# A transformer step in two blocks on one core: recurrence by halves, fused attention maximum, earlier bias split, more held expert weights, first modulation by feature halves

## The chip, the cores and the metric

The kernel runs on one core of a Trainium2 chip. A core has a matrix engine (PE in the profile; its weight loads are PEld), a vector engine (DVE), an activation engine (ACT), a general engine (POOL) and a queue engine that issues transfers (SP, in the profile SPq). They run side by side and wait for each other by semaphores; 16 DMA engines move data between HBM and the on-chip memory. The metric is the device time of one execution in microseconds (us), less is better.

## The reference, cut to what matters

All data are float32, 256 tokens of 1024 features. The first block: modulation vectors from a condition, a projection to 2840 columns, two kinds of attention, a residual, and a mixture of 32 experts in which each token goes to four.

```python
mod = silu(c) @ ada_w + ada_b            # six vectors of 1024: shift, scale, gate, twice
h = rms_norm(x, ln1_g) * (1 + sc1) + sh1
z = h @ w_in                             # 1024 -> 2840
# compressed, selected and windowed attention on 8 heads, blockwise attention on 8 heads
s = softmax(q @ k.T * scale - slope * distance)
x = x + g1 * (concat(outputs) @ w_out)
u = h2[toks] @ w1[e] + b1[e]             # per expert; g_, lin = halves of u, clipped at 7
y = ((lin + 1) * g_ * sigmoid(1.702 * g_)) @ w2[e] + b2[e]
```

The second block puts 16 tokens ("meta") in front, so that it works on 272 columns, and has stick-breaking attention, an MLP, a gated linear recurrence and another MLP. The meta tokens are dropped at the end. The recurrence:

```python
gate = gelu(x @ w_in[:, :1024]);  u = causal_conv(x @ w_in[:, 1024:])
r, i = sigmoid(u @ w_rg + b_rg), sigmoid(u @ w_ig + b_ig)
log_a = (-8 * softplus(-lam)) * r;  a = exp(log_a)
bt = sqrt(-expm1(2 * log_a)) * (i * u)
h[t] = a[t] * h[t-1] + bt[t];  out = (h * gate) @ w_out
```

## The kernel before

Activations lie feature-major: a feature chunk of 128 on the partitions, tokens along the row. The program of each engine is written out by hand, in order, and nothing else sets the order. Every weight goes through a ring of four slots of 2 MB (`ring`), filled by SP in the order of `A_LOADS` (first block), then expert by expert, then `B_LOADS` (second block); SP waits until the slot's last reader is done before it issues the next load, and everything behind that load waits too.

**Front.** SP loads the condition `c`, `x`, and the modulation weights as four loads of 256 rows by 2048 columns (`ada`), then `w_in` in six column chunks. PE transposes `x`, multiplies modulation rows (L750), turns them (L758), and DVE makes the normalized, modulated input `hn` (L1608 to L1618). Only then does the projection begin: twelve products (v = 0 to 11, six chunks by two token halves, L795), each over all eight feature chunks. The first four need `w_in` columns 0 to 1023.

**Attention.** 12 units. For each, PE scores 768 columns into two PSUM banks (L885), DVE adds the distance bias into `scores` (L1742), takes four row maxima in two reductions (L1745, L1746), ACT exponentiates with them as bias (L1434), DVE makes factors from the sums (L1754 to L1760), POOL scales (L592), PE transposes (L895 to L899) and weighs the values (L914 to L919). Between these PE does the rest of the modulation (L750).

**Between attention and experts.** When the attention is done, SP loads held weights (L486) and ACT issues the loads of the expert biases. PE multiplies by `w_out` (L994), DVE adds the residual and makes the second `hn` (L1789, L1792), tokens are ranked, the first expert's rows are gathered (L1076). Meanwhile POOL splits the bias `b1` in three bfloat16 parts (L624 to L629); the first expert pass waits for that (`split_ready`).

**Experts.** A pass takes up to 64 tokens of an expert: PE adds the bias (L1111), multiplies four parts of `w1` (L1122, `w1_parts` counts them), gathers the next rows (L1076), scatters the last result (L1094), and multiplies two halves of `w2` (L1153). An expert has 12 MB of weights in six loads. Part 0 of experts 20, 24 and 28 does not come then: it has been loaded beforehand to a spare place, and POOL copies it into the ring slot. An expert with more than 64 tokens takes a second pass on the same weights.

**Recurrence.** PE makes eight recurrence inputs, the first gate input (L1316), 16 gate products (L1330), and then the other seven gate inputs (L1316), each of 272 columns. DVE, ACT and POOL make `a`, the square root and the gelu on whole tensors of eight chunks (128x2176) or on four (128x1088), DVE runs a scan per chunk (L2061) and gates it (L2070), and PE's output product (L1182, `dense`) waits for chunk k of the gated result at its k-th step (`lru_y`).

Of the kernel before, what the change touches and what calls it, by code (L numbers as in the profile page):

```python
# [33 lines left out]
BF16 = mybir.dt.bfloat16  # L34
# [6 lines left out]
P = 128  # L41
# [13 lines left out]
NEG = -1e30  # L55
FLAT = 30.0
# [13 lines left out]
A_LOADS = ([("ada", 0, k) for k in range(4)]  # L70
           + [("in", 0, c) for c in range(6)] + [("cmp", 0, 0)]
# [9 lines left out]
DMAS_OF = {"wout": 4, "gates": 2}  # L81
# [3 lines left out]
HELD = (20, 24, 28)  # L85
# [41 lines left out]
def a_freed(n):  # L127

    kind, layer, c = A_LOADS[n]
    return {"ada": ("mod_parts", 4 * layer + c + 1), "in": ("z_done", 2 * (c + 1)),  # L130
            "cmp": ("cmp_hidden", 1), "wout": ("wout_done", 4 * (c + 1))}[kind]
# [64 lines left out]
class Memory:  # L196

    def __init__(self, nc, ctx):
# [67 lines left out]
        self.OT = a.take(C, T)  # L267

# [30 lines left out]
        self.b2 = a.take(D)  # L299
        self.b1 = a.take(2, FF)  # L300
        self.b1parts = a.take(2, FF, dt=BF16)
# [21 lines left out]
        w2_at = ARENA - 864 - 2 * SLOT  # L323
        held_at = w2_at - len(HELD) * SLOT
        assert a.at <= held_at
        self.held = Area(arena, held_at).take(len(HELD), SLOT)
        self.w2 = Area(arena, w2_at).take(2, SLOT)
# [44 lines left out]
z_done z_copied doubled heads_ssq heads_root heads_normed gates_ready  # L372
# [3 lines left out]
scored biased maxed exped factored scaled flipped flipped_dve flipped_act o_parts o_copied  # L376
# [11 lines left out]
gate_tanh_in gate_tanh_in2 gate_tanh gate_tanh2 u_ready r_ready lam_in lam_out a_in a_exp mult_in mult_root lru_y  # L388
# [4 lines left out]
class Signals:  # L393

    def __init__(self, nc, ctx):
        self.sem = {name: ctx.enter_context(nc.semaphore(name)) for name in SEMAPHORES}
        self.loaded = [ctx.enter_context(nc.semaphore(f"loaded{s}")) for s in range(RING)]
        self.held_loaded = [ctx.enter_context(nc.semaphore(f"held_loaded{j}")) for j in range(len(HELD))]
# [6 lines left out]
def program_sync(nc, sp, m, s, a):  # L406
# [5 lines left out]
    def source(kind, layer, c):  # L412

        if kind == "ada":
            src = a["ada_w"][0, 2 * P * c:2 * P * (c + 1), 2048 * layer:2048 * (layer + 1)]
            return [(slice(0, P), 4096, 2048, src.rearrange("(k p) n -> p k n", p=P))]
        if kind == "in":
# [48 lines left out]
    for n, load_of in enumerate(A_LOADS):  # L466
        if n >= RING:
            wait_for(a_freed(n - RING))
        load(A_AT[n][0], load_of, s.loaded[A_AT[n][0]])
        if n == 0:  # L470
# [12 lines left out]
    def load_held(j):  # L483

        src = a["exp_w1"][0, HELD[j], 0:2 * P, :]
        sp.dma_start(m.held[:, j, :], src.rearrange("(p k) n -> p (k n)", p=P)).then_inc(s.held_loaded[j], 16)  # L486
# [12 lines left out]
    for part in range(PASS_LOADS):  # L499
# [6 lines left out]
        elif part == 4:  # L506
            sp.wait_ge(s["wout_done"], C)
# [12 lines left out]
    for held in HELD + (EXPERTS,):  # L520
        with sp.Fori(begin, held) as expert:
            load_expert(expert)
        if held < EXPERTS:
            load_expert(held, from_part=1)
        begin = held + 1

# [7 lines left out]
def program_gpsimd(nc, pool, m, s, a):  # L534
# [42 lines left out]
    for t in range(2):  # L577
        src = m.z[:, t, Z_KC:Z_KS].rearrange("p (g d) -> p g d", g=4).unsqueeze(2).to_broadcast([P, 4, 2, DH])
        g.tensor_copy(m.twice[:, t].rearrange("p g (c d) -> p g c d", c=2), src).then_inc(s["doubled"], 1)
    for u in range(UNITS):  # L580
        if u == 8:
            pool.wait_ge(s["heads_normed"], 5)
            pool.wait_ge(s["mod_ready"], 2)
# [32 lines left out]
    link(g.memset(m.wtile, 0.0))  # L616
    link(g.memset(m.b2[EXPERTS:64, :], 0.0))
    link(g.memset(m.b2[64:P, :], 0.0))
    g.memset(m.b1parts[96:P, :, :], 0.0).then_inc(s["pool_moe"], 1)
    pool.wait_ge(s["pool_moe"], 3)  # L620

    pool.wait_ge(s["bias_loaded"], 64)
    link(g.tensor_copy(m.b1parts[0:96, :, :], m.b1[0:96, :, :]))  # L624
    for q in (1, 2):
        for r in range(q, 3):
            rows = slice(32 * r, 32 * r + 32)
            link(g.tensor_tensor(m.b1[rows], m.b1[rows], m.b1parts[rows], ALU.subtract))
            last = g.tensor_copy(m.b1parts[rows], m.b1[rows])  # L629
            if (q, r) == (2, 2):  # L630
                last.then_inc(s["split_ready"], 1)
            else:
                link(last)
# [5 lines left out]
    for j, expert in enumerate(HELD):  # L639
# [3 lines left out]
        seen = m.b1[0:32, 0, 0:1]  # L643
        link(g.tensor_tensor(seen, seen, seen, ALU.subtract))
        pool.wait_ge(s.held_loaded[j], 16)
# [1514 lines left out]
```

## Time and profile before

| | us |
|---|---|
| median of 3 runs | 1906.66 (1902.97 to 1910.16) |
| profiled execution | 1906.46 |
| its span, first to last instruction | 1904.7 |
| PE busy | 1803.5 |
| DVE, ACT, POOL busy | 513.6, 252.6, 122.8 |

Busy time alone says little here: the stages have different limits. Times in the rows below are us from the start of the span. In a timeline row the numbers are the start, the length, the engine and line, the operation, what is written and read, the count, and in brackets how long the engine was idle before and what released it. The mean granted clock of PE is 0.991 of full.

### The profile page before, as it was taken

What the parts mean: (1) busy time and instruction counts of PE and PEld (TensorE: products, weight loads), DVE (VectorE), ACT (ScalarE), POOL (GpSimd) and SP (SyncE); (2) the same over time, 40 slices, a digit from 0 to 9 for tenths busy, and PEclk for the clock granted to TensorE, in tenths of its full rate; (3) what the DMA queues carried; (4) which work ended last, traced back from release to release, by engine and by line L of the source; (5) the groups of instructions that cost most, each with busy time, mean ns of one, the idle gap of its engine ahead of it and who ended that gap; (6) DMA issues with size and microseconds to landing.
All of it is one profiled execution on the core that took longest, in us unless ns stands there. A gap on an engine that the chain in (4) does not pass through costs nothing.

```text
span 1904.7 us, 21694 instructions
## 1 busy us (share of the span) xinstructions
PE 1803.5 (95%) x8583; PEld 1033.1 (54%) x8584; DVE 513.6 (27%) x1032; ACT 252.6 (13%) x519; POOL 122.8 (6%) x172
## 2 busy tenths in 40 slices
PE   6989899999999899899999989989999999899998
PEld 3545633333333333233333326867888888788887
DVE  1247532232313222222323313133110006611000
ACT  1125200011001001001001002022110003111000
POOL 3004500000000000100101001000000000200000
PEclk8999999999999999999999999999999999999999
DMA  9558899979999999999999997321344333434430
GB/s 361 178 229 266 320 407 428 428 305 428 428 428 429 428 429 427 428 429 428 429 428 428 428 428 289 133 89 45 133 158 152 133 132 111 176 133 160 150 132 23
DMA packets 93092, 547.38 MB, mean 287 GB/s; under 512 B 5906, under 2 KB 9186, under 8 KB 65298
## 3 DMA queue, kind: packets, MB, share of 16 engines
q1 hardware_dynamic: 92850, 545.75, 71.4%
q10 hardware_dynamic: 192, 0.92, 0.2%
q8 instruction: 37, 0.61, 0.1%
q14 instruction: 13, 0.11, 0.0%
HBM read 545.60 MB, written 1.05 MB: 287 GB/s over the span
## 4 chain that ended last, share of the span: by engine, by line
PE 66%; DMA 27%; DVE 4%; SPq 1%; issue 1%; POOL 1%; ACT 1%; DVEq 0%; POOLq 0%; ACTq 0%
DMA ring<-in_exp_w 26%; PE ps L1182 21%; PE ps L1122 13%; PE ps L1281 12%; PE ps L1153 5%; PE ps L795 4%; PE ps L1076 1%; PE ps L994 1%; PE ps L1094 1%; PE ps L1316 1%; PE ps L1233 1%; DMA ring<-in_w_in 1%; DVE arena L2061 1%; SPq L480 0%; PE ps L750 0%
## 5 line engine op out<-in xcount | busy, mean ns | idle before, releaser
L1122 PE MATMUL ps<-ring,arena 128*64 128x512 f32 x2112 | 470.7, 595 | 45.0 <-DMA ring<-in_exp_w 44.9
L1182 PE MATMUL ps<-hn,ring 128*128 128x272 f32 (+1 forms) x1536 | 346.5, 388 | 0.0
L1122 PEld LDWEIGHTS ps<-ring,arena 128*64 128x64 f32 x2112 | 150.0, 137 | 346.0 <-issue 247.1
L1182 PEld LDWEIGHTS ps<-hn,ring 128*128 128x128 f32 x1536 | 291.8, 190 | 53.3
L1153 PE MATMUL ps<-arena,hn 128*64 128x512 f32 x1056 | 233.9, 595 | 3.5
L1281 PE MATMUL ps<-arena,ring 128*128 128x272 f32 (+1 forms) x1024 | 228.5, 386 | 1.1 <-DVE arena L2011 1.1
L1281 PEld LDWEIGHTS ps<-arena,ring 128*128 128x128 f32 x1024 | 194.3, 190 | 35.0 <-DVE arena L2011 1.9
L1153 PEld LDWEIGHTS ps<-arena,hn 128*64 128x64 f32 x1056 | 75.3, 137 | 140.9 <-issue 140.6
L1912 DVE TENSOR_SCALAR sq<-ps 128x512 f32<-128x512 f32 x33 | 22.8, 692 | 346.9 <-PE ps L1122 346.9
L1824 DVE TENSOR_SCALAR sq<-arena,rstd 128x64 f32<-128x64 f32 x68 | 19.1, 324 | 304.3 <-PE ps L1122 303.6
L1362 ACT ACTIVATE hn<-ps 128x512 f32<-128x512 f32 (+1 forms) x99 | 52.0, 525 | 308.4 <-PE ps L1153 212.2
L1475 ACT ACTIVATE sq<-sq 128x512 f32<-128x512 f32 x33 | 20.8, 629 | 536.0 <-DVE sq L1912 536.0
L1951 DVE TENSOR_TENSOR xT<-ps,xT 128x272 f32<-128x272 f32 (+1 forms) x32 | 13.9, 433 | 261.8 <-PE ps L1281 217.9
L1843 DVE TENSOR_TENSOR arena<-ps,arena 128x512 f32<-128x512 f32 x132 | 81.5, 680 | 7.3 <-PE ps L1094 7.3
L795 PE MATMUL ps<-ring,hn 128*128 128x512 f32 (+1 forms) x192 | 78.5, 571 | 2.3 <-DMA ring<-in_w_in 2.3
L2011 DVE SCALAR_TENSOR_TENSOR arena<-ps,rstd 128x272 f32<-128x272 f32 (+1 forms) x64 | 27.5, 433 | 182.3 <-PE ps L1182 182.2
L676 POOL TENSOR_TENSOR sq<-sq 128x272 f32<-128x272 f32 (+1 forms) x34 | 25.4, 746 | 640.3 <-ACT sq L1495 639.8
L1094 PE MATMUL ps<-hn 64*128 64x512 f32 x264 | 65.6, 615 | 0.7 <-issue 0.7
L1182 PE MATMUL ps<-arena,ring 128*128 128x272 f32 (+1 forms) x256 | 59.6, 395 | 6.4 <-DVE arena L2070 5.8
L1076 PE MATMUL ps<-arena,sq 128*64 128x512 f32 x272 | 65.4, 601 | 0.0
L795 PEld LDWEIGHTS ps<-ring,hn 128*128 128x128 f32 x192 | 37.0, 194 | 42.6 <-issue 40.6
L1182 PEld LDWEIGHTS ps<-arena,ring 128*128 128x128 f32 x256 | 49.2, 194 | 16.4 <-DVE arena L2070 4.0
(365 smaller groups left out, 1231.1 us busy)
## 6 DMA issues: line engine op xcount, KB each, us to landing
ring<-in_exp_w SPq DMA_DIRECT2D x125, 2048.0 KB, 23.5
arena<-in_exp_w SPq DMA_DIRECT2D x67, 2048.0 KB, 21.6
ring<-in_mlp_w_up SPq DMA_DIRECT2D x16, 2048.0 KB, 7.5
ring<-in_mlp_w_down SPq DMA_DIRECT2D x16, 2048.0 KB, 7.8
ring<-in_ada_w SPq DMA_DIRECT2D x12, 2048.0 KB, 10.5
ring<-in_sb_w_qkv SPq DMA_DIRECT2D x6, 2048.0 KB, 14.0
ring<-in_w_in SPq DMA_DIRECT2D x5, 2048.0 KB, 11.0
ring<-in_lru_w_in SPq DMA_DIRECT2D x4, 2048.0 KB, 7.9
```

Of the source, the lines that this page charges most:

```text
L676: add = g.tensor_tensor(m.sq[:, 0, lo:TT], m.sq[:, 0, lo:TT], m.sq[:, c, lo:TT], ALU.add)
L795: last = mm(bank(v % 4)[:, 0:w], m.hn[:, k, META + P * t:META + P * t + P], wt[:, k, :], start=(k == 0), stop=(k == C - 1))
L1076: last = mm(bank(0)[64 * h:64 * h + 64, :], m.sel[:, t, :], m.h2[:, t, 512 * h:512 * h + 512], start=(t == 0), stop=(t == 1))
L1094: mm(bank(TOKEN_BANKS[n]), m.selz[rows, h, P * t:P * t + P], m.y[rows, :], start=True, stop=True).then_inc(s["scattered"], 1)
L1122: last = mm(bank(2 + part)[64 * h:64 * h + 64, :], lhs, w[:, k % 2, at:at + 512], start=False, stop=(k == C - 1))
L1153: last = mm(bank(5)[64 * h:64 * h + 64, :], m.aT[:, q, 64 * half:64 * half + 64], w[:, q, 512 * h:512 * h + 512], start=(half == 0 and q = ...
L1182: last = mm(bank((n0 + q) % 8)[:, lo:TT], w[:, k, P * q:P * q + P], act[:, k, lo:TT], start=(k == 0), stop=(k == C - 1))
L1281: last = mm(bank(4 * half + q)[:, lo:TT], w[:, k, P * q:P * q + P], m.mlp[:, f, lo:TT], start=(f == 0), stop=(f == 31))
L1362: f(dst, src, ACT.Copy, scale=scale).then_inc(s[name], 1)
L1843: v.tensor_tensor(part, bank(TOKEN_BANKS[n]), part, ALU.add).then_inc(s["added"], 1)
L1912: v.tensor_scalar(m.g, bank(2), 7.0, None, ALU.min).then_inc(s["g_ready"], 1)
L2011: v.scalar_tensor_tensor(m.relu[:, n % 8, lo:TT], bank(n % 8)[:, lo:TT], 0.0, m.rstd[:, lo:TT], ALU.max, ALU.mult).then_inc(s["b_relu"], 1)
```

## The change

- **Front.** The four modulation loads become eight (`mod`): two halves of the rows by two halves of the features of both vectors, in 512-column pieces, and `w_in` columns 0 to 1023 are loaded in two halves of the rows. The loads go mod 0, mod 1, w_in rows 0 to 511, mod 2, mod 3, w_in rows 512 to 1023. The first four products are made over feature chunks 0 to 3 first, then over 4 to 7, in banks 0 to 3.
- **Attention.** Four instructions `tensor_tensor_reduce` (two of 256 columns, two of 128) subtract the scores from the negated bias and keep the minimum; ACT takes them with scale -1.
- **Biases.** `b1` and `b2` are loaded by SP behind the last `w_in` chunk, and POOL makes the split in halves before its first scaling. The first load of `w2` waits for the split as well.
- **Held weights.** Part 0 of experts 18, 22 and 26, and half of that of expert 30 (the other half comes with its turn). A single semaphore for all.
- **Recurrence.** Everything between the gate products and the output product goes by halves of four chunks; the first square of the gelu and that of `a` go to ACT, POOL does nothing here; gate inputs and gelu have 256 columns, without the meta tokens. The first output product goes over chunks 0 to 3 for all four output chunks, then over 4 to 7.

The core of the diff:

```diff
-A_LOADS = ([("ada", 0, k) for k in range(4)]
-           + [("in", 0, c) for c in range(6)] + [("cmp", 0, 0)]
+A_LOADS = ([("mod", 0, 0), ("mod", 0, 1), ("in", 0, 0), ("mod", 0, 2), ("mod", 0, 3)]
+           + [("in", 0, c) for c in range(1, 6)] + [("cmp", 0, 0)]
-HELD = (20, 24, 28)
+HELD = ((18, 4096), (22, 4096), (26, 4096), (30, 2048))
...
+    def load_rest(j):
+        expert, words = HELD[j]
+        ...
+        wait_for(pass_freed(last, 0))
+        sp.dma_start(m.ring[:, r, words:SLOT], src[:, words:SLOT]).then_inc(s.rest_loaded, 16)
...
+    def project_half(v, wt, half, chunks):
+        for k in chunks:
+            if v == 0:
+                pe.wait_ge(s["h_ready"], 4 * half + k + 1)
+            ...
+    project_half(0, halves[0], 0, range(4))
+    for v in (1, 2):
+        pe.wait_ge(s["x_placed"], v)
+        project_half(v, halves[0], 0, range(4))
+        first_modulation(v + 1)
+    pe.wait_ge(s["x_placed"], 3)
+    project_half(3, halves[0], 0, range(2))
+    turn_first_modulation(1)
+    project_half(3, halves[0], 0, range(2, 4)).then_inc(s["in_first"], 1)
...
-            v.tensor_tensor(sc, m.ps[:, b:b + 2, 0:384], m.bias[:, i, :].rearrange("p (h k) -> p h k", h=2),
-                            ALU.add).then_inc(s["biased"], 1)
-            v.tensor_reduce(m.nmax[:, u % 3, 0:2], sc[:, :, 0:256], AX.X, ALU.max, negate=True)
-            v.tensor_reduce(m.nmax[:, u % 3, 2:4], sc[:, :, 256:384], AX.X, ALU.max,
-                            negate=True).then_inc(s["maxed"], 1)
+            for q, (h, at, n) in enumerate(((0, 0, 256), (1, 0, 256), (0, 256, P), (1, 256, P))):
+                last = v.tensor_tensor_reduce(sc[:, cols], bank(b + h)[:, at:at + n], bias[:, cols], -1.0, LARGEST,
+                                              ALU.add, ALU.min, m.nmax[:, u % 3, q:q + 1])
...
-            last = mm(bank(n)[:, 0:TT], w[:, k, P * q:P * q + P], m.hn[:, k, :], ...)
+            last = mm(bank(n)[:, META:TT], w[:, k, P * q:P * q + P], m.hn[:, k, META:TT], ...)
...
-        dense(N_LOUT + 4 * c, B_LOUT + c, m.hs, lo=META, made=("lru_y", 0) if c == 0 else None)
+    for kh in range(2):
+        for q in range(4):
+            for k in range(4 * kh, 4 * kh + 4):
+                if q == 0:
+                    pe.wait_ge(s["lru_y"], k + 1)
```

PE in the front of the program, before: `L750` and `L786` are modulation products, `L758` and `L795` of before and after their transposes, `L795` before and `L843` after the projection.

```order
L750 MATMUL ps<-ring,arena 32x512 x8
L740 MATMUL ps<-sq,ones 128x256 x8
L723 MATMUL ps<-ident,arena 128x104
L750 MATMUL ps<-ring,arena 32x512 x24
L758 MATMUL ps<-ident,arena 128x128 x4
L795 MATMUL ps<-ring,hn 128x512 x16
```

And the same place after:

```order
L786 MATMUL ps<-ring,arena 32x256 x16
L795 MATMUL ps<-ident,arena 128x128 x2
L843 MATMUL ps<-ring,hn 128x512 x8
L786 MATMUL ps<-ring,arena 32x256 x16
L843 MATMUL ps<-ring,hn 128x512 x4
L786 MATMUL ps<-ring,arena 32x256 x16
L843 MATMUL ps<-ring,hn 128x512 x2
L795 MATMUL ps<-ident,arena 128x128 x2
L843 MATMUL ps<-ring,hn 128x512 x10
```

Products of the projection now stand ahead of half of the modulation.

DVE in the recurrence, before, from the multiplication of the input gate (`L2049`) to the first gated chunks (`L2070`); `L2061` is the scan, `L2029` a gate input, `L2058` the weighting by the root:

```order
L2049 TENSOR_TENSOR arena<-arena 128x2176
L2052 TENSOR_TENSOR arena<-arena 128x2176
L2054 SCALAR_TENSOR_TENSOR arena<-arena 128x2176
L2029 TENSOR_TENSOR arena<-ps,rstd 128x272 x2
L2058 TENSOR_TENSOR arena<-arena 128x2176
L2061 SCALAR_TENSOR_TENSOR arena<-arena 128x272 x4
L2061 SCALAR_TENSOR_TENSOR arena<-arena 128x272 x4
L2080 SCALAR_TENSOR_TENSOR arena<-arena 128x1088
L2070 SCALAR_TENSOR_TENSOR arena<-arena 128x272 x4
```

After, from the same multiplication (`L2166`) to the second pair of scans (`L2178`); `L2175` is the weighting, `L2183` the cube, `L2142` a gate input:

```order
L2166 TENSOR_TENSOR arena<-arena 128x1088 x2
L2170 SCALAR_TENSOR_TENSOR arena<-arena 128x1088
L2142 TENSOR_TENSOR arena<-ps,rstd 128x256
L2170 SCALAR_TENSOR_TENSOR arena<-arena 128x1088
L2175 TENSOR_TENSOR arena<-arena 128x1088
L2178 SCALAR_TENSOR_TENSOR arena<-arena 128x272 x4
L2183 SCALAR_TENSOR_TENSOR arena<-arena 128x4x256
L2175 TENSOR_TENSOR arena<-arena 128x1088
L2178 SCALAR_TENSOR_TENSOR arena<-arena 128x272 x2
```

The square of `a` (L2052) is gone from DVE, and the scans of the first half stand ahead of the weighting of the second.

## Rows read from the trace of the kernel before

**Rows 1.** Timeline of PE and its weight loads, 0 to 114 us.
```profile
21.61 1.92 PE L750 MATMUL ps<-ring,arena 128*32 128x512 f32 x16 [1.00 <-DMA ring<-in_ada_w]
34.88 15.77 PE L795 MATMUL ps<-ring,hn 128*128 128x512 f32 x32 [2.31 <-DMA ring<-in_w_in]
...
59.53 54.49 PE L795 MATMUL ps<-ring,hn 128*128 128x512 f32 x141
60.82 0.19 PEld L795 LDWEIGHTS ps<-ring,hn 128*128 128x128 f32 x1 [0.24 <-issue]
```

**Rows 2.** Windows; last three columns: granted PE clock, DMA busy share, GB/s.
```profile
15.00:20.00 5.00, 5.00 (x34) 3.45 (x33) 0.73 (x1) 0.47 (x1) 4.32 (x9) 1.00 1.02 423
...
35.00:40.00 5.00, 5.00 (x8) 2.17 (x9) 0.70 (x3) 0.00 (x0) 0.00 (x0) 0.65 1.06 381
```

**Rows 3.** Timeline of the attention units, PE, ACT and DVE.
```profile
165.41 0.92 PE L885 MATMUL ps<-arena 64*128 64x256 f32 x8
...
169.08 0.92 PE L885 MATMUL ps<-arena 64*128 64x256 f32 x8
...
177.40 0.96 DVE L1742 TENSOR_TENSOR arena<-ps,arena 128x768 f32<-128x768 f32 x1 [0.92 <-PE ps L885]
178.39 0.69 DVE L1745 TENSOR_REDUCE arena<-arena 128x2 f32<-128x512 f32 x1
179.00 0.41 DVE L1746 TENSOR_REDUCE arena<-arena 128x2 f32<-128x256 f32 x1
...
143.72 0.19 ACT L1434 ACTIVATION_READ_ACCUMULATOR arena<-arena 128x1 f32 x1
```

**Rows 4.** Timeline between attention and first expert, DVE, POOL and PE.
```profile
199.31 0.35 DVE L1792 TENSOR_SCALAR hn<-xT,affine 128x256 f32<-128x256 f32 x1
...
205.90 4.06 POOL L628 TENSOR_TENSOR arena<-arena 32x2048 f32<-32x2048 f32 x1
...
206.66 3.45 DVE L1792 TENSOR_SCALAR hn<-xT,affine 128x256 f32<-128x256 f32 x1
...
221.76 1.26 DVE L1808 COPY arena<-arena 128x8 f32<-128x8 f32 x1
...
223.51 1.48 DVE L1812 TENSOR_SCALAR arena<-arena 128x64 f32<-128x64 f32 x1
...
227.37 3.05 PE L1076 MATMUL ps<-arena,sq 128*64 128x512 f32 x8
```

**Rows 5.** Timeline of SP: issues of expert weights.
```profile
237.41 11.26 SPq L493 DMA_DIRECT2D ring<-in_exp_w  x4
...
399.59 10.53 SPq L493 DMA_DIRECT2D ring<-in_exp_w  x4
```

**Rows 6.** Chain that ended last, in order of time: start, length, what.
```profile
774.65 3.68 PE ps L1122 x16
778.48 25.51 DMA ring<-in_exp_w
...
857.90 3.68 PE ps L1122 x16
```

**Rows 7.** Timeline of the recurrence, PE, ACT and DVE.
```profile
1611.96 25.83 PE L1316 MATMUL ps<-hn,ring 128*128 128x272 f32 x112
1641.03 1.97 PE L1182 MATMUL ps<-arena,ring 128*128 128x256 f32 x8 [3.25 <-DVE arena L2070]
...
1621.16 2.02 ACT L1554 ACTIVATE arena<-arena 128x2176 f32<-128x2176 f32 x1 [1.97 <-DVE arena L2054]
...
1625.96 7.48 DVE L2061 TENSOR_TENSOR_SCAN arena<-arena 128x272 f32<-128x272 f32 x4
...
1634.79 2.99 DVE L2061 TENSOR_TENSOR_SCAN arena<-arena 128x272 f32<-128x272 f32 x4
...
1637.82 1.29 DVE L2080 SCALAR_TENSOR_TENSOR arena<-arena 128x1088 f32<-128x1088 f32 x1
...
1659.85 0.42 DVE L1951 TENSOR_TENSOR xT<-ps,xT 128x256 f32<-128x256 f32 x1 [2.64 <-PE ps L1182]
```

More of the change, by code:

```diff
@@ L55 @@
 NEG = -1e30
+LARGEST = 3e38
 FLAT = 30.0
@@ L519, in program_sync @@
     begin = 1
-    for held in HELD + (EXPERTS,):
+    for j, (held, words) in enumerate(HELD):
         with sp.Fori(begin, held) as expert:
             load_expert(expert)
-        if held < EXPERTS:
-            load_expert(held, from_part=1)
+        if words < SLOT:
+            load_rest(j)
+        load_expert(held, from_part=1)
         begin = held + 1
+    with sp.Fori(begin, EXPERTS) as expert:
+        load_expert(expert)
     sp.wait_ge(s["w1_parts"], passes * 4)
@@ L615, in program_gpsimd @@
     link(g.memset(m.wt, 0.0))
[L616 to L619, printed above, removed]
+    link(g.memset(m.seen, 0.0))
+    g.memset(m.wtile, 0.0).then_inc(s["pool_moe"], 1)
     pool.wait_ge(s["pool_moe"], 3)
[L623 to L633, printed above, removed]
     pool.wait_ge(s["split_ready"], 1)
@@ L741, in sum_squares, with first_modulation, turn_first_modulation @@
         last.then_inc(s["norm_summed"], 1)
+    def first_modulation(part):
+        h, rows = part // 2, part % 2
+        w = a_slot(A_LOADS.index(("mod", 0, part))).rearrange("p (n k f) -> p n k f", n=2, f=512)
+        for k in range(4):
+            for r in range(4):
+                last = mm(bank(MOD_BANK[0])[32 * r:32 * r + 32, 256 * h:256 * h + 256], m.condR[:, 4 * rows + k, :],
+                          w[:, r // 2, k, 256 * (r % 2):256 * (r % 2) + 256],
+                          start=(rows == 0 and k == 0), stop=(rows == 1 and k == 3))
+        last.then_inc(s["mod_parts"], 1)
+    def turn_first_modulation(h):
+        pe.wait_ge(s["mod_rows"], h + 1)
+        for q in range(2):
+            at = 256 * h + P * q
+            last = turn(bank(MOD_TURN_BANK[0])[:, at:at + P], m.modrow[:, at:at + P], ident)
+        last.then_inc(s["mod_turned"], 1)
     def modulation_half(group, half):
@@ L2073, in program_vector, with gated @@
+    def gated(chunks, number):
+        hs = m.hs[:, chunks, META:TT]
+        v.scalar_tensor_tensor(hs, hs, 0.5, m.g3[:, chunks, META:TT], ALU.mult, ALU.mult).then_inc(s["lru_y"], number)
+    entered(0, first)
+    entered(1, second)
+    gate_input(1)
+    complement(0, first)
+    gate_input(2)
+    complement(1, second)
+    gate_input(3)
+    weighted(0, first)
     for c in range(4):
         scan(c)
+    cubed(first, 1)
     gate_input(4)
-    cubed(4)
-    for c in range(4, C):
+    weighted(1, second)
@@ L2092, in program_vector @@
+    for c in (6, 7):
+        scan(c)
+    gelu(first, 1)
+    gated(first, 4)
+    gate_input(6)
+    cubed(5, 3)
+    gelu(4, 2)
+    gate_input(7)
+    cubed(6, 4)
+    gated(4, 1)
+    cubed(7, 5)
+    for c in range(5, C):
+        gelu(c, c - 2)
+        gated(c, 1)
     residual(N_LOUT, 56, PC_NMLP + C, META)
```

289 lines of the change are left out of this document (178 added, 111 removed).

## Prediction

> **What bounds the kernel now.** I read the chain of waits first, then the timelines at the places of the change. Four stretches matter. Until 34.88 us the loads bound: the first product of the projection was released by a transfer [rows 1]. From there to 59.53 + 54.49 = 114.0 us PE is never idle. The attention is bound by PE too: units start 169.08 - 165.41 = 3.67 us apart [rows 3], while DVE's add and two maxima end 179.41 - 177.40 = 2.0 us after they begin. Then comes a run of short steps to the first expert. From the first expert on, the transfers bound, but not at once: part 0 of expert 1 is issued at 237.41, when PE has used expert 0's. The six loads of an expert take 778.48 + 25.51 - 774.65 = 29.3 us, PE's pass less. An expert with two passes lets the ring fill up, so nothing is issued until 399.59, when its last pass frees a slot [rows 5], and from there to the last expert DMA is the limit [rows 6]. So whatever moves the issue at 237.41 moves the whole rest, and behind 399.59 only bytes count. In the second block PE is the limit except in the recurrence, where it waits for DVE from 1637.8 to 1641.03 and again inside the product that follows [rows 7].
>
> **Front.** A 2 MB load takes 2.097 MB / 423 GB/s = 4.96 us with long rows, and 2.097/381 = 5.50 with rows of 2 KB as `w_in` has [rows 2]; the new modulation loads have rows of 2 KB, +0.54 us each. The third load of 2 MB was used at 21.61 [rows 1]. It is now w_in's first half, behind two modulation loads: 22.7 us. `hn` of chunks 0 to 3 needs mod 1 (17.2 to 17.8 by the same count), 1.9 us of products, the turn and some short DVE steps, about 22.5, so neither is far behind the other. PE then has, with an instruction each 0.19 + 0.24 = 0.43 us [rows 1] and two to a product: v = 0 and 1, 16 instructions, 6.9 us, to 29.6; mod 2, 1.9 us (as the 1.92 of rows 1), to 31.5; v = 2, 3.4 us, to 35.0. Mod 3 is the fifth load; the fifth landed at 34.88, with four modulation loads in front or in it now +2.1: 37.0. So PE waits 2 us, then mod 3, the other turn and v = 3, 5.9 us together, to 42.9. The last half of w_in has landed at 37.0 + about 5.2 = 42.2, and DVE's second half of `hn` follows the turn 1.7 us before PE is done with v = 3. From 42.9 PE has 13.8 us of second halves and what it had behind the first four products before. Those began at 34.88 with 15.77 + 13.8 us, so the stage then ended 114.0 - 34.88 - 29.6 = 49.5 us after them. It ends at 42.9 + 13.8 + 49.5 = 106.2: 7.8 us earlier. Bounds: 3 if each load comes later than counted and PE's clock falls while it waits (the first 32 instructions took 15.77 instead of 13.8 us at a granted clock of 0.65, rows 1 and 2), and 9.5 if 2 KB rows cost nothing and PE doesn't wait for mod 3. Value 7.8.
>
> The bias loads (0.9 MB, about 2 us) go behind the last w_in chunk, between loads that PE needs only tens of us later. POOL's split, three subtractions of 4.06 us [rows 4] and four casts of half that, some 21 us, begins when the biases have landed, about 70 us. POOL has nothing to do there, and DVE only the head norms, which PE needs after 106. Price nothing; without that cover the head norms would be late by one POOL instruction, 2 us. The trace shows what such a meeting costs: beside POOL's 4.06 us a DVE instruction took 3.45 instead of 0.35 us [rows 4]. 
>
> **Attention.** Out go 0.96, 0.69 and 0.41 us (2.0 from start to end); in come two fused instructions of 256 and two of 128 columns, each with a read of its accumulator. Not in the trace. At one element per cycle like the add (0.96 us for 768), four instructions come to 0.96 + 3 x 0.15 = 1.4 us, and four reads add 0.1 to 0.19 each, the latter being ACT's [rows 3]: 1.8 to 2.2 us. At half that rate 0.8 more. PE's next scores now wait for all of it instead of the add alone, but of the unit before last, 3.67 us ahead. So in the steady state nothing changes while DVE's share of a unit, with about 1 us of factors and copy, stays under 3.67. At the start PE waits for the first unit's factors, which stand behind two units of DVE work: twice the difference. Value 0, bounds -0.6 (gain) and +5 (half rate: 3.9 us a unit, 12 x 0.25, and 1.8 at the start).
>
> **To the first expert.** With POOL's split gone, DVE's 3.45 becomes 0.35, of which PE felt 0.45; the copy at 221.76 and the compare at 223.51 (1.26 and 1.48 us, for 0.2 us of work each) stand between the logits and the ranks: 2.3 us. One delayed `hn` chunk before the logits, 0.35. Together 3.1. PE's idle time ahead of the gather shrinks by 2.3, and the gather took 3.05 us there [rows 4], at full clock it would be 8 x 0.43 us by two side by side, 1.7: up to 1.3 more. Value 3.7, bounds 1.5 and 4.5. Behind the attention DMA has 1 MB more of held weights and 0.9 MB less of biases: nothing. Expert 0's last load then ends shortly before the earlier issue of expert 1 (237.41 - 3.7 counted from the end of attention), so the gain passes on.
>
> **Held weights.** Two passes with one held load took 857.90 - 803.99 = 53.9 instead of 58.7 us: 4.9 for 2 MB [rows 6]. Half a load more: 2.4. POOL's copy and SP's extra wait lie in front of a slot that has long been free. Bounds 0 and 2.4. Front to first expert, the held bytes are loaded under PE's output product.
>
> **Recurrence.** Gate inputs have 256 of 272 columns: 25.83 x 16/17 = 24.3 us for seven, and 0.2 on the first, so PE is done at 1611.8 + 24.3 = 1636.1. DVE: the root of the first half can be had at about 1622.5 (ACT has six half instructions of about 1.05 us, a table load and one half root, from 1612.6; all of it came at 1623.2 before, rows 7). Then weighting 1.3, four scans 3.0, cube 1.2, gate inputs 0.9, the second weighting 1.3, two scans 1.5, cube 0.4, two scans 1.5, gelu 1.2, gating 1.2 and small gaps: 14.1, to 1636.7. A half instruction is the 1.29 of rows 7, a scan 2.99/4. The first four scans took 7.48 beside POOL; POOL is now idle. PE starts its output product at 1636.7, and has 4 x 3.45 = 13.8 us in it, with the second half of the inputs (gated by about 1642) needed only after 6.9: done at 1650.5. Before it ended at 1659.85. Value 9.3; bounds 6 (DVE 3 us later) and 10 (PE never waits).
>
> **Sum.** 7.8 + 0 + 3.7 + 2.4 + 9.3 = 23.2. The profiled execution took 1906.46 us, 1.8 more than its span, and the median is 1906.66, the same within 0.01%: 1883.3 us.
>
> **Rivals.**
> 1. *The front gives little.* Smaller rows and the small parameter loads keep PE waiting at mod 2, mod 3 and the second half, and its clock down. For: 381 against 423 GB/s, and the clock of 0.65. Against: PE has 10 us of work between them. Front 3, or held weights 0: 1887 to 1889.
> 2. *DVE becomes the bound of the attention*, by the half rate above: 1889. The Trainium skill (Vector Engine (DVE) Microarchitecture Reference, Points that are easy to get wrong) says that one form of instruction runs at half throughput with two sources of 4-byte data in SBUF, for want of a port for the accumulator. Here one source is in PSUM, and the trace has two such sources at 1088 elements in 1.29 us, full rate, but without an accumulator. By the rule's letter the fused instruction stays at full rate, by its spirit it may not.
> 3. *The other side.* The fused instruction is slow by itself, a fixed price each. It decides from 5.6 us per unit of DVE time on (3.67 + 23.2/12), that is 1.2 us for each of the four, against 0.4 expected. At 1.5 us each, a unit takes 6.9 us, 12 x 3.3 = 39 us more: 1922. Against: no DVE instruction of this size takes that unless POOL blocks it.
> 4. *The change doesn't reach the recurrence's end*: DVE still late, since ACT's table loads and squares stand in its chain: gain 4 instead of 9: 1889.
>
> **Chances.** Forecast (1879 to 1887) 0.60; rivals 1, 2 and 4, and two of them together (1887 to 1896) 0.31; two or three and something unseen (1897 to 1916) 0.06; rival 3, 0.03. About 0.5%, 9.5 us, is what a measurement can tell from no change, so faster is below 1897: 0.90, same 0.07, slower 0.03. Range: 1877 (all upper bounds give 26 to 29) to 1894.
>
> **What would show it.** The projection ends at 106; PE's first L843 (projection) at about 22.7, clock near full. Attention units 3.67 apart, fused instructions 0.3 to 0.45 us. No DVE instruction over 1 us between output product and ranks. The interval of 29.4 in the experts unchanged, 53.9 in three places and 56.3 at the end. PE idle under 1 us before the output product of the recurrence. I am wrong if the attention period grows, or if the four stretches shrink by less than 12 us together.

## The result, and the profile after

The changed kernel took 1878.07 us (median of 4 runs, 1877.43 to 1881.61), the kernel before 1907.43 beside it: ratio 0.9852, 95% interval 0.9829 to 0.9875. Run again later beside nine runs of before, it took 1879.26: 0.9852, 0.9837 to 0.9867. The medians differ by 29.4 us the first time and by 27.7 the second.

The profiled execution was the slowest of its four (1881.61 us, span 1880.0). A second profile of the same kernel (that of "after again" below) has a span of 1877.7. Both are used here, as "after" and "after, second". Where they differ, the difference belongs to no edit. The gains in the table add up to the differences of the spans, 24.7 and 27.0 us.

| stretch, us | before | after | after, second | gain | forecast |
|---|---|---|---|---|---|
| start to first head turn (the projection ends 0.8 earlier) | 114.80 | 107.95 | 106.63 | 6.9, 8.2 | 7.8 |
| to first attention scores | 19.78 | 19.81 | 19.79 | 0 | 0 |
| first scores to output product | 53.26 | 50.75 | 49.93 | 2.5, 3.3 | 0 |
| output product to first expert product | 45.34 | 40.86 | 40.86 | 4.5 | 3.7 |
| to the issue of expert 1 | 4.23 | 3.81 | 3.81 | 0.4 | 0 |
| issue of expert 1 to issue of expert 6 | 162.18 | 163.35 | 162.96 | -1.2, -0.8 | 0 |
| from there to the last first-layer product | 742.45 | 739.94 | 740.61 | 2.5, 1.8 | 2.4 |
| to the gate products of the recurrence | 462.58 | 462.72 | 462.24 | -0.1, 0.3 | 0.2 |
| gate products to the last residual behind the output product | 55.23 | 45.86 | 45.87 | 9.4 | 9.1 |
| to the end | 244.85 | 244.95 | 245.00 | -0.1 | 0 |

**Front.** Timeline of PE, after, answering to [rows 1]; L843 is the projection, L786 the modulation:

```profile
19.92 0.44 PE L795 MATMUL ps<-ident,arena 128*128 128x128 f32 x2 [0.62 <-DVE arena L1706]
23.97 8.63 PE L843 MATMUL ps<-ring,hn 128*128 128x512 f32 x16 [3.61 <-DMA ring<-in_w_in]
32.53 1.93 PE L786 MATMUL ps<-ring,arena 128*32 128x256 f32 x32
34.39 3.70 PE L843 MATMUL ps<-ring,hn 128*128 128x512 f32 x8
38.02 1.93 PE L786 MATMUL ps<-ring,arena 128*32 128x256 f32 x32
```

The same place in the second profile:

```profile
22.47 7.10 PE L843 MATMUL ps<-ring,hn 128*128 128x512 f32 x16 [2.26 <-DMA ring<-in_w_in]
29.50 1.93 PE L786 MATMUL ps<-ring,arena 128*32 128x256 f32 x32
31.37 3.70 PE L843 MATMUL ps<-ring,hn 128*128 128x512 f32 x8
36.70 1.93 PE L786 MATMUL ps<-ring,arena 128*32 128x256 f32 x32 [1.63 <-DMA ring<-in_ada_w]
```

In the first, w_in came 1.5 us later, PE idled 3.6 us, and the next 16 instructions took 8.63 instead of 7.10 us. Its windows (the third number from the end is the granted clock) show that the clock was low there, and one more fall of the clock, in the second block's attention:

```profile
20.00:25.00 5.00, 1.39 (x4) 0.67 (x5) 3.11 (x7) 0.00 (x0) 3.03 (x5) 0.86 1.04 392
25.00:30.00 5.00, 5.00 (x11) 2.23 (x10) 0.00 (x0) 0.00 (x0) 0.00 (x0) 0.80 1.14 284
...
1250.00:1255.00 5.00, 5.00 (x16) 2.93 (x14) 1.06 (x1) 0.78 (x2) 0.00 (x0) 0.50 0.01 3
```

The length of the gap doesn't decide whether the clock falls. Two of the runs below had the same gap at the same time, and it fell in one ("early modulation group", first line) and not in the other ("biases late", second line):

```profile
22.59 8.80 PE L843 MATMUL ps<-ring,hn 128*128 128x512 f32 x16 [2.18 <-DVE hn L1717]
...
22.52 7.10 PE L811 MATMUL ps<-ring,hn 128*128 128x512 f32 x16 [2.18 <-DVE hn L1690]
```

**Attention.** Units stand 160.56 - 156.88 = 3.68 us apart, as in [rows 3]. One unit's maxima on DVE, after:

```profile
157.85 0.42 DVE L1858 CUSTOM_DVE_ANT_0 arena<-ps,arena 128x256 f32<-128x256 f32 x1 [1.86 <-PE ps L958]
158.20 0.08 DVE L1858 DVE_READ_ACCUMULATOR2_ANT arena<- 128x1 f32 x1
158.20 0.42 DVE L1858 CUSTOM_DVE_ANT_0 arena<-ps,arena 128x256 f32<-128x256 f32 x1
158.55 0.08 DVE L1858 DVE_READ_ACCUMULATOR2_ANT arena<- 128x1 f32 x1
158.55 0.28 DVE L1858 CUSTOM_DVE_ANT_0 arena<-ps,arena 128x128 f32<-128x128 f32 x1
...
158.76 0.28 DVE L1858 CUSTOM_DVE_ANT_0 arena<-ps,arena 128x128 f32<-128x128 f32 x1
```

The next instruction starts 0.35 us after a wide one and 0.21 after a narrow one, with the read of the accumulator inside that. The four end 1.2 us after they begin, against 2.0 before.

**To the first expert.** DVE and PE, after, answering to [rows 4]:

```profile
208.28 0.35 DVE L1905 TENSOR_SCALAR hn<-xT,affine 128x256 f32<-128x256 f32 x1
...
211.70 0.17 DVE L1921 COPY arena<-arena 128x8 f32<-128x8 f32 x1
...
212.36 0.19 DVE L1925 TENSOR_SCALAR arena<-arena 128x64 f32<-128x64 f32 x1
...
214.69 1.94 PE L1149 MATMUL ps<-arena,sq 128*64 128x512 f32 x8 [0.20 <-DVE arena L1939]
```

The copy and the compare take 0.36 us together instead of 2.74, the gather 1.94 instead of 3.05. The gather's part comes from the clock, which was low while it ran before and full after. The window of the gather before, and that of its end after (the one ahead of it has 1.00 too):

```profile
225.00:230.00 5.00, 4.87 (x20) 2.39 (x20) 1.86 (x11) 1.81 (x3) 0.00 (x0) 0.66 0.98 419
```

```profile
215.00:220.00 5.00, 3.34 (x20) 1.43 (x18) 2.96 (x12) 0.58 (x1) 0.00 (x0) 1.00 1.00 419
```

PE had idled 2.9 us for DVE's compare before it fell. In the ten other runs with the early split the gather took 1.94 us each time.

**Held weights.** Chain of waits, after, answering to [rows 6]. Two passes, of expert 18 (part 0 held; POOL's first copy of a held part runs at 722.67) and of expert 19, take 786.00 - 732.12 = 53.9 us together:

```profile
732.12 3.65 PE ps L1195 x16
...
786.00 3.68 PE ps L1195 x16
```

The pairs with the other two whole held parts take 53.9 and 54.0 us, the last pair, with the half part, 1126.47 - 1070.14 = 56.3.

**Recurrence.** Timeline of PE and DVE, after, answering to [rows 7]; L2175 weights by the root, L2178 scans, L2192 gates the first half:

```profile
1596.52 24.34 PE L1389 MATMUL ps<-hn,ring 128*128 128x256 f32 x112
1620.96 14.05 PE L1414 MATMUL ps<-arena,ring 128*128 128x256 f32 x64
...
1607.42 1.28 DVE L2175 TENSOR_TENSOR arena<-arena 128x1088 f32<-128x1088 f32 x1
1608.74 3.00 DVE L2178 TENSOR_TENSOR_SCAN arena<-arena 128x272 f32<-128x272 f32 x4
...
1619.59 1.23 DVE L2192 SCALAR_TENSOR_TENSOR arena<-arena 128x1024 f32<-128x1024 f32 x1
```

DVE is done with the first half at 1620.82, PE with the gate inputs at 1620.86; the trace shows no wait of PE there.

### The profile page after: what moved, and what is told of

Its sections match the earlier page's. It is cut to its first block, busy times and chain, and to the rows that moved or that the text cites. A ratio compares the mean times of both kernels' runs of the same rounds, so it can differ in the third digit from the quotient of the medians.

```text
span 1880.0 us, 21926 instructions
## 1 busy us (share of the span) xinstructions
PE 1794.5 (95%) x8647; PEld 1033.0 (55%) x8648; DVE 493.9 (26%) x1092; ACT 257.3 (14%) x529; POOL 120.2 (6%) x182
## 4 chain that ended last, share of the span: by engine, by line
PE 67%; DMA 29%; DVE 2%; issue 1%; POOL 1%; ACT 0%; SPq 0%; DVEq 0%; POOLq 0%
DMA ring<-in_exp_w 28%; PE ps L1255 20%; PE ps L1195 13%; PE ps L1354 12%; PE ps L1226 5%; PE ps L871 3%; PE ps L843 2%; PE ps L1067 1%; PE ps L1389 1%; PE ps L1149 1%; PE ps L1167 1%; DMA ring<-in_w_in 1%; PE ps L1414 1%; PE ps L1306 1%; PE ps L805 1%
## 5 line engine op out<-in xcount | busy, mean ns | idle before, releaser
L1354 PE MATMUL ps<-arena,ring 128*128 128x272 f32 (+1 forms) x1024 | 228.5, 386 | 1.1 <-DVE arena L2124 1.1
L1354 PEld LDWEIGHTS ps<-arena,ring 128*128 128x128 f32 x1024 | 194.3, 190 | 35.0 <-DVE arena L2124 1.9
L1572 ACT ACTIVATE sq<-xT 128x272 f32<-128x272 f32 (+1 forms) x40 | 16.2, 422 | 274.9 <-DVE xT L2064 274.9
L1611 ACT ACTIVATE arena<-arena 128x272 f32<-128x272 f32 (+1 forms) x64 | 26.9, 423 | 187.5 <-DVE arena L2124 187.5
L871 PE MATMUL ps<-ring,hn 128*128 128x512 f32 (+1 forms) x128 | 48.9, 544 | 0.0
```

Of the source, the lines that this page charges most:

```text
L871: last = mm(bank(v % 4)[:, 0:w], m.hn[:, k, META + P * t:META + P * t + P], wt[:, k, :], start=(k == 0), stop=(k == C - 1))
L1354: last = mm(bank(4 * half + q)[:, lo:TT], w[:, k, P * q:P * q + P], m.mlp[:, f, lo:TT], start=(f == 0), stop=(f == 31))
L1611: f(m.mlp[:, n, lo:TT], m.relu[:, n % 8, lo:TT], ACT.Square).then_inc(s["mlp_ready"], 1)
```

## The experiments

Each ratio is against the kernel before on the same chip. The unchanged "after" has 0.9852 by this measure, and 0.0010 is 1.9 us. Since runs of one kernel differ by 1 to 4 us (those of the kernel before by up to 7), and the interval of a ratio is 2.5 to 3 us to either side, the verdicts rest on stretches of the profile, and the ratios only have to agree.

### Undoing one part at a time

**Front as before.** `A_LOADS` with four `ada` loads of 256 rows, `w_in` whole, the projection behind all of the modulation.

> The changed kernel with the old front: four modulation loads of 256 rows by 2048 columns, then w_in whole, the projection begun after all modulation. Theory (the parts add, the front gave 6.9 us): the projection ends at 114.0 instead of 107.2, everything up to the second block lies 6.9 us later (expert 1 issued at about 230), time 1885. Rival (the later start is caught up by the transfer stream, which is what binds from expert 1 on): expert 1 is issued at 230, but its loads then come without contention and the experts end only 4 to 5 us later, time 1882.

Measured 1886.88 us, ratio 0.9896 (0.9881 to 0.9911). First head turn at 115.47, expert 1 issued at 229.62:

```profile
229.62 11.66 SPq L516 DMA_DIRECT2D ring<-in_exp_w  x4
```

The head turn is 7.5 and 8.8 us later than in the two profiles of after, the issue of expert 1 6.4 and 8.6, the issue of expert 6 (392.82) 6.3 and 8.8, the last expert product (1132.75) 6.3 and 8.2. The 1.1 us between 7.5 and 6.4 lie at the first two scores, which are 4.08 us apart here and 5.15 in the first profile of after, because the clock was low for a shorter time. The transfers take nothing back: the rival fell.

**Maxima as before.**

```diff
-            for q, (h, at, n) in enumerate(...):
-                last = v.tensor_tensor_reduce(sc[:, cols], ..., ALU.add, ALU.min, m.nmax[:, u % 3, q:q + 1])
+            v.tensor_tensor(sc, m.ps[:, b:b + 2, 0:384], ..., ALU.add).then_inc(s["biased"], 1)
+            v.tensor_reduce(m.nmax[:, u % 3, 0:2], ...)
+            v.tensor_reduce(m.nmax[:, u % 3, 2:4], ...)
```

> The changed kernel with the old add and two row maxima in place of the four fused instructions. Theory (DVE's shorter group helps PE at the start, at one wait in the middle and behind the last scores): the time from the first scores to the output product grows by 2.5 us, of which 1.5 us is there by the sixth unit; up to 1 us of it is lost again in the transfer stream, time 1880 to 1881. Rival (the fused maximum changes nothing, as forecast, and the 2.5 us came from something else between the two kernels, for instance the biases loaded and split elsewhere): stretch and time unchanged, 1878.

Measured 1880.18 us, 0.9865 (0.9850 to 0.9881). The distances between the scores of successive units tell more than the sum:

| from unit | 1 | 2 | 3 | 4 | 5 | 6 | 7 | 8 to 11 | last scores to output product |
|---|---|---|---|---|---|---|---|---|---|
| before | 5.15 | 2.41 | 4.25 | 3.63 | 3.67 | 3.89 | 3.94 | 14.91 | 11.41 |
| old maxima in after | 5.02 | 1.85 | 4.31 | 3.57 | 3.67 | 3.89 | 3.95 | 14.90 | 11.42 |
| after | 5.15 | 1.85 | 3.51 | 3.49 | 3.67 | 3.89 | 3.67 | 14.91 | 10.61 |
| after, second | 4.34 | 1.85 | 3.51 | 3.49 | 3.67 | 3.89 | 3.67 | 14.90 | 10.61 |

The fused maxima are worth 0.8 us behind unit 3, 0.1 behind unit 4, 0.3 behind unit 7 and 0.8 behind the last scores, 2.0 in all, and nothing in any other unit. The rest of the 2.5 and 3.3 us lies in the first two distances, where the maxima play no part: PE's clock is low there, for longer or shorter (0.50 to 0.91 in windows of 5 us of these four profiles). First scores to output product is 52.6 us here, 1.8 and 2.7 more than in the two profiles of after, so the rival fell. The old group in this run, 2.0 us long:

```profile
139.76 0.96 DVE L1857 TENSOR_TENSOR arena<-ps,arena 128x768 f32<-128x768 f32 x1
140.76 0.69 DVE L1860 TENSOR_REDUCE arena<-arena 128x2 f32<-128x512 f32 x1
141.36 0.41 DVE L1861 TENSOR_REDUCE arena<-arena 128x2 f32<-128x256 f32 x1
```

**Recurrence as before** (whole tensors, 272 columns, POOL in it).

> The changed kernel with the old recurrence (whole tensors, 272 columns, POOL at work). Theory: the stretch from the first gate input to the end of the output product grows by 9.6 us and nothing else moves, time 1888. Rival (part of it came from the clock or from loads, so that the old form beside the new loads costs less): 4 to 7 us, time 1882 to 1885.

Measured 1889.36 us, 0.9913 (0.9900 to 0.9927). PE and DVE of it:

```profile
1607.46 7.48 DVE L2149 TENSOR_TENSOR_SCAN arena<-arena 128x272 f32<-128x272 f32 x4
...
1622.54 2.53 PE L1260 MATMUL ps<-arena,ring 128*128 128x256 f32 x8 [3.25 <-DVE arena L2158]
1625.63 1.22 PE L1260 MATMUL ps<-arena,ring 128*128 128x256 f32 x2 [0.57 <-DVE arena L2158]
1627.76 13.53 PE L1260 MATMUL ps<-arena,ring 128*128 128x256 f32 x55 [0.91 <-DVE arena L2158]
```

The waits of PE are back (3.25 us as in [rows 7], then 0.57 and 0.91), and the four scans take 7.48 us beside POOL. From the gate products to the last residual it is 55.00 us, 9.1 more than after. Of these, 1.5 us are the wider gate inputs (25.83 us for 24.34) and 4.7 the three waits; the other 2.9 lie in the output product, where the granted clock is 0.50 from 1625 to 1630. It is 1.00 throughout this stretch of after, so a part of the gain is that PE, without the wait, keeps its clock. The run undoes the halves, the narrower columns and the rest for POOL together; what each did for DVE alone is not told apart. The rival (4 to 7 us) fell; the time is 1.4 us above the 1888 expected.

**Biases late, held weights 20, 24, 28.**

> The changed kernel with the late load and split of the expert biases and with the old held weights (part 0 of experts 20, 24, 28). Theory: output product to first expert product takes 45.3 instead of 40.9 us (DVE instructions of 1 to 3.5 us are back), the issue of expert 1 comes 4.5 us later, but the transfer stream gives back 1 to 1.3 of it; the held weights cost 2.5 us more; together 5.7 to 7 us, time 1884 to 1885. Rival (what comes before the issue of expert 1 is passed on in full, and the held half load is worth nothing): 4.5 us, time 1882.5.

Measured 1887.36 us, 0.9900 (0.9884 to 0.9915). Output product to first expert product 45.39 us, with the same long rows as in [rows 4]; the gather runs at the low clock again (granted 0.66 from 215 to 220):

```profile
210.06 1.25 DVE L1894 COPY arena<-arena 128x8 f32<-128x8 f32 x1
...
211.80 1.48 DVE L1898 TENSOR_SCALAR arena<-arena 128x64 f32<-128x64 f32 x1
...
215.41 3.57 PE L1117 MATMUL ps<-arena,sq 128*64 128x512 f32 x8 [0.20 <-DVE arena L1912]
```

The issue of expert 6 and the last expert product:

```profile
389.21 10.63 SPq L503 DMA_DIRECT2D ring<-in_exp_w  x4
...
1131.54 3.65 PE L1163 MATMUL ps<-ring,arena 128*64 128x512 f32 x16 [1.24 <-DMA ring<-in_exp_w]
```

That is 742.33 us, against 742.45 before, 739.9 to 740.1 in the first profile of after and the three runs above, and 740.6 in its second, which hold 18, 22, 26 and half of 30. In the six other runs of the next section it is 739.8 to 740.0. So the early biases are worth 4.5 us and the half load 2.4; the two parts were undone in one run and are told apart by where they show. The time, 1887.36, is 2.4 us above the forecast, and the stretches explain 6.9 of the 9.1 us by which the ratio differs; the rest is within the interval. A loss in the transfer stream, 1.2 us between expert 1 and expert 6, can't be pinned on an edit: this distance is 163.67 here with the old biases and held weights, 163.20 with the old front, and 162.38 to 164.01 in the ten profiles with neither. The one profile of before, 162.18, is a little below all of these.

### What differs from run to run, and what comes of it

In the profiles of the changed kernel and its variants the granted clock falls at three places above all, where PE idles now and then: in the front at 20 to 30 us (in four of the eight profiles with the new front and no idle products), around the first scores (in all but one), and in the second block's attention, where PE idles 1.6 and then 2.7 us. There it fell in every profile with those gaps except "maxima as before" (in "early modulation group" at 1242.2 already, between the two gaps, in the others in or behind the second). That one run took 459.6 us from the last expert product to the gate products, the profiles with a fall 461.2 to 462.7, after being the longest: the fall costs 1.6 to 3.1 us. Its first accumulation behind the same gap ran at full speed:

```profile
1250.28 0.99 PE L1306 MATMUL ps<-arena 128*128 128x432 f32 x2 [2.73 <-DVE arena L2104]
```

Versions that put work into these gaps:

**Idle products in the front.**

```diff
     pe.wait_ge(s["x_placed"], 4)
+    for _ in range(8):
+        mm(bank(0)[:, 0:T], ident, m.xT[:, 0, META:TT], start=True, stop=True)
```

> The changed kernel with eight more products of 128x256 (about 1.8 us at full clock, result unused) on PE while it waits for the first half of w_in after 20.4 us. Theory (the 3.6 us of idle lower the granted clock to 0.8 in the next 10 us, and the first 16 products then take 8.63 instead of 7.1 us): with the gap filled to 1.8 us or less the clock stays at 1.00, the 16 products take 7.1 us, the projection ends about 1.5 us earlier, time 1876.5. Rival (the lateness is that of the transfer, and the clock fell for another reason): 16 products at 8.6 us, time 1878.

Measured 1879.18 us, 0.9855 (0.9840 to 0.9870). They took 3.62 us, since a product of 256 columns is two instructions of 0.23; the next 16 took 7.13 us:

```profile
20.32 3.62 PE L836 MATMUL ps<-xT,ident 128*128 128x256 f32 x16
23.84 7.13 PE L845 MATMUL ps<-ring,hn 128*128 128x512 f32 x16
```

The clock stays up, as the theory said, and did so in all three runs with such products, as it did in four of the eight without. But the time doesn't fall to the 1876.5 expected. The first head turn comes at 106.91 us on the mean of the three profiles with idle products (106.84 to 106.95) and at 106.91 on the mean of the eight without (106.14 to 107.95): they gain nothing there. Two things take the gain away. They end 1.4 us behind the moment at which the load was there in the second profile of after, which had 7.10 without them. And what the clock gives back is lost again at the next load: of the two runs with the gap of 2.18 us shown above, the one with the full clock then waited 1.64 us for mod 3, the other not at all, and their head turns are at 106.69 and 106.74.

**Early modulation group.**

```diff
     last.then_inc(s["cmp_scored"], 1)
+    modulation_half(1, 4)
```

> The changed kernel with one group of eight modulation products moved from behind the first scores to ahead of them, where PE idles 1.5 us for DVE (126.2 to 127.8). Theory (PE is late with the second unit's scores because 16 modulation products at half clock stand in between, 5.15 us from first to second scores): the second unit comes 1 to 1.8 us earlier and everything after it as well, time 1876.5. Rival (DVE or ACT bound the start of the attention, so the later units stay where they are): the first gap shrinks and the next ones grow, time 1878.

Measured 1877.33 us, 0.9842 (0.9828 to 0.9855). The first three scores are 1.85 us apart, and then the fourth is 4.78 behind the third:

```profile
126.53 0.92 PE L959 MATMUL ps<-arena 64*128 64x256 f32 x8 [0.53 <-DVE arena L1817]
127.38 1.07 PE L805 MATMUL ps<-ring,arena 128*32 128x512 f32 x8
128.38 0.92 PE L959 MATMUL ps<-arena 64*128 64x256 f32 x8
...
133.99 0.33 PE L969 MATMUL ps<-ident,arena 128*128 128x128 f32 x1 [1.84 <-POOL arena L647]
```

First to last scores 38.11 instead of 40.14 and 39.32 us: 1.2 to 2.0 gained, 1.3 of the 3.3 at the first unit being given back at the fourth, where PE waits for POOL's scaling. Theory and rival are each right by half. It is also the one profile in which the clock held around the first scores. In the two later versions with the same edit it fell, and the first distance is 2.58 and 3.45 us, first to last scores 37.85 and 38.74.

**Early score in the second block.**

```diff
     b_score(1)
+    b_score(2)
     for i in range(9):
...
-        if i + 2 < 8:
+        if 1 <= i and i + 2 < 8:
             b_score(i + 2)
```

> The changed kernel with the third head's scores of the second block's attention moved ahead of the first accumulation, into 2.7 us in which PE is idle (1246.6 to 1249.3). Theory (the products fill idle time, 1.5 us, and by keeping PE at work they avert the fall of the clock to 0.5 that cost up to 3.1 us here in some of the runs so far): the stretch from the last expert product to the recurrence takes 459.3 - 1.5 = 457.8 us if the clock falls all the same, 454.7 if it doesn't, time 1873.5 to 1876.5. Rival (PE then waits for DVE's second softplus or ACT's exponential): 459.3 minus nothing, time 1878.

Measured 1875.35 us, 0.9833 (0.9819 to 0.9846). PE's first accumulation (L1306), after and then here:

```profile
1249.34 1.80 PE L1306 MATMUL ps<-arena 128*128 128x432 f32 x2 [2.73 <-DVE arena L2102]
```

```profile
1246.89 0.99 PE L1306 MATMUL ps<-arena 128*128 128x432 f32 x2 [1.21 <-DVE arena L2103]
```

The gap shrinks from 2.73 to 1.21 us and the clock stays at 1.00. From the last expert product to the gate products it is 458.0 us, against 462.7 in after (4.7 less) and 459.6 in "maxima as before", where the clock had held (1.5 less): 1.5 for the filled gap, and 3.1 for the clock against after, 1.6 to 3.1 against all profiles with a fall. The two later versions with this edit took 458.0 us too, at full clock. The 454.7 of the expectation took the 3.1 off 459.3, about what the stretch takes with the clock held, so it counted the gain of the clock twice.

**All three.**

> The changed kernel with all three: the eight idle products in the front, the early modulation group, the early score. Theory (they lie in three different stretches and add, and the transfer stream of the experts passes the first two on): 1.5 + 1.5 + 1.5 to 4.6, time 1870.5 to 1873.5. Rival (what comes before the experts is taken back by the transfers): only the third counts, time 1875 to 1876.5.

Measured 1874.01 us (1873.33 to 1874.15), 0.9826 (0.9813 to 0.9840). That is 0.5 us above the theory's range and under the rival's in every run. By the ratios, the three edits alone gave -0.6, 1.9 and 3.6 us against after, and together 5.0: they add, as far as ratios can tell.

**After again.**

> The changed kernel once more, unchanged, beside two others on one chip, to see how far the first profile of it (span 1880.0) was a late one. Theory (transfers in the front and the granted clock ahead of the scores and in the second block's attention differ from run to run by 1 to 3 us each): the span is between 1875 and 1880 and each difference to the first profile lies in those three places, time 1877 to 1879. Rival: the difference is spread evenly over the run.

Measured 1879.26 us, 0.9852 (0.9837 to 0.9867). The first scores are 1.3 us earlier and the distance to the second is 0.8 us less, 2.1 of the 2.3 us. The clock was low in the second block's attention again, for 0.5 us less in all. From the issue of expert 6 on, the transfers took 0.7 us more than in the first profile, and 0.4 less ahead of it, so not every difference lies in the three places that were named. The span is in the expected range, the median 0.3 us above it.

**All three, with four idle products.**

> As the version with all three edits, but with four idle products in the front instead of eight, since eight took 3.6 us and ended just at the transfer. Theory (what helps is that the gap is shorter, not that it is gone): the first 16 products take 7.1 us and can begin at 22.6 where the load is early, time 1873 to 1874, 3.5 to 5 us under the changed kernel. Rival (with 1.8 us of idle left the clock falls as without the products): 16 products at 8.6 us, time 1874.5 to 1876.

Measured 1874.13 us (1873.53 to 1875.85), 0.9828 (0.9815 to 0.9841), on the same chip as "after again": 5.1 us less. The 16 products took 7.10 us. They began at 23.62, since PE turned the first modulation 1.6 us later here than in after (21.58 for 19.92), and the idle products left no gap; whether a shorter gap would have kept the clock was so not tested. The time lies between theory and rival. This version and "all three" are the fastest seen, and no run of either is as slow as the fastest of the changed kernel.

**More work on DVE in the attention.**

```diff
+            for n in range(2):
+                v.tensor_reduce(m.more[:, 2 * u + n, :], m.ps[:, b:b + 2, 0:384], AX.X, ALU.max)
             sc, bias = m.scores[:, u % 2, :], m.bias[:, i, :]
```

> The changed kernel with two more reductions of the scores in PSUM (768 columns each, about 1 us each, results unused) ahead of the four fused instructions of each attention unit. Theory (PE bounds the attention while DVE has less than 3.67 us a unit; now DVE has 1.2 + 2.0 + 1.1 = 4.3): units 4.3 us apart, the time from the first scores to the output product goes from 50.8 to about 60, total 1886 to 1888. Rival (DVE's work counts at the start, at one unit and at the end alone, 2.4 times the difference, as the old maxima did): 50.8 + 4.8 = 55.6, total 1883.

Measured 1886.15 us, 0.9890 (0.9875 to 0.9906). PE's scores of two successive units:

```profile
157.45 0.92 PE L959 MATMUL ps<-arena 64*128 64x256 f32 x8
...
161.42 0.92 PE L959 MATMUL ps<-arena 64*128 64x256 f32 x8
```

From the fourth to the last scores the mean distance is 33.77/8 = 4.22 us, after it is 29.63/8 = 3.70; first scores to output product 58.4 us. The theory's 4.3 and 60 nearly hold, the rival's 55.6 doesn't: with this work DVE bounds the attention. From 145 to 170 us it is busy 4.4 to 5.0 us of every 5, at full granted clock, and PE is not busy all the time any more.

## Why the prediction was right, and where it wasn't

- **The time.** Forecast 1883.3, measured 1878.07, inside the range of 1877 to 1894 but near its lower end. Two terms of the sum were too small: attention by 2.0, the way to the experts by 0.8. The upper bounds of the terms add up to 9.5 + 0.6 + 4.5 + 2.4 + 10 = 27.0 us and not to "26 to 29", so they end at 1879.7: the measured time is inside the range only by what the range had beyond its own bounds, and that part is luck. The profile of before sat at its median; that of after did not. Its span is 24.7 us under the span of before, the medians differ by 29.4, and the second profile by 27.0.
- **Front, 7.8.** 6.9 and 8.2 in the two profiles. The w_in half landed at 23.97 and 22.47 for the 22.7 counted. "v = 0 and 1, 16 instructions, 6.9 us" holds where the clock does (7.10). The wait of 2 us for mod 3 was 1.63 in one profile and none in the other, where the low clock had filled it.
- **Attention, 0 with a bound of 0.6 for a gain.** This is the term that failed: it measured 2.0, outside its bounds. I added each accumulator read to its instruction (1.8 to 2.2 us); they run inside it, 1.2 us. And I let the group count only at the start, twice. It counts once (0.8 us) behind unit 3, 0.1 behind unit 4, 0.3 behind unit 7, and once more (0.8) behind the last scores. That the last one shows because no later unit hides DVE's group is my reading of the order; the run shows the places and the sizes.
- **To the first expert, 3.7.** 4.5. The copy and the compare gave 2.4 for 2.3, the gather 1.1 for "up to 1.3", of which the sum had only 0.6.
- **Held weights, 2.4.** 2.4 against the old set in the same kernel. Distances of 29.4, 53.9 and 56.3 us stand as forecast.
- **Recurrence, 9.3.** 9.4 behind the gate products, where 9.1 was counted, and 9.1 by undoing. DVE needed 13.4 us from the first weighting (1607.42) to the gated first half, for 14.1 counted, and PE arrived at the same moment. That a PE that doesn't wait keeps its clock was in the sum unnoticed: the working took the output product at full clock.
- **The rivals.** 1 (front 3) fell. 2 (half rate) and 3 (slow fused instruction) fell: a step of 0.35 us for 256 columns is near the add's rate, 0.96/3 = 0.32. The Trainium skill (Vector Engine (DVE) Microarchitecture Reference, Points that are easy to get wrong) gives half throughput for one form of instruction with two sources in SBUF that aren't bfloat16. By the letter of that rule the trace agrees: one source is in PSUM here, and the rate isn't halved. No run has the case that the rule is about. What rival 2 feared does exist: in "more work on DVE" DVE was the bound, with some 4.0 us of work a unit (my estimate, 23.76 us busy out of 25, times 4.22). Where between that and about 2 us, which the same sum gives for after (8.26 out of 15, times 3.70), it becomes the bound wasn't measured. 4 fell: PE waits 0.
- **What stays open.** Why w_in's first half lands anywhere from 22.5 to 24.0, and why the five experts' transfers take 162.2 to 164.0 us. Why the clock falls in one run and not in another behind the same gap. And why the issue of expert 1 comes 0.4 us earlier behind the first expert product: it does so in all four runs that undo a part, so it belongs to none of the parts that were undone.

## What to carry to other kernels

In a pipeline in which one engine is the bound, a shorter step of another can be worth nothing per turn and still count once while the pipeline fills and once at its end (0.8 us each here, for a difference of 0.8); count both ends. Work that is ready anyway belongs into the gaps of the matrix engine, not only for its own length (1.5 us here) but for the clock of what stands behind the gap (1.6 to 3.1 us), which falls in some runs and not in others. It helps only where the engine is the bound behind the gap: in the front, the next load took back what the clock gave. Compare stretches between fixed instructions of several profiles, and take the spread of an untouched stretch for the error of the touched ones.

## What the runs showed of the hardware

- The fused subtract-and-minimum took 0.42 us for 256 columns and 0.28 for 128, the next instruction started after 0.35 and 0.21, and the read of the accumulator (0.08) cost nothing.
- The granted clock fell to 0.50 around the 2.73 us gap in the second block's attention in nine of the ten profiles without the early score (in one of them ahead of the gap), and in none of the three with it, where the gap is 1.21 us. The one without a fall took 1.6 to 3.1 us less there.
- In the front, a gap of 2.2 us was followed by a fall in two profiles and by none in two others: 8.80 or 7.10 us for the same 16 instructions.
- The gather ran in 1.94 us at full clock in 11 profiles, and in 3.05 and 3.57 us in the two in which PE had idled 2.9 us ahead of it.
- Four scans of 272 columns took 7.48 us beside POOL and 3.00 without it.
